# Group A attention: plain fp32 probabilities and values, weighed on two 64-column tiles of TensorE, without remainders

## The reference, cut to what matters

```
def _gqa_blocked(q, k, v):            # 8 query heads, 2 key/value heads, head size 64, blocks of 128 queries
    sc = jnp.einsum('bqkgd,bskd->bkgqs', qblk, k, preferred_element_type=jnp.float32) * scale
    p = jax.nn.softmax(sc, axis=-1).astype(v.dtype)
    return jnp.einsum('bkgqs,bskd->bqkgd', p, v)
```

## Time and profile before

| | before |
|---|---|
| median of 3 runs | 2302.78 us (2302.01 to 2313.93) |
| the profiled execution | 2301.58 us, its span 2299.8 us |
| mean granted PE clock | 0.982 of full speed |
| PE, DVE, ACT, POOL busy | 2200.8, 1622.3, 803.5, 291.9 us |
| group A, from the first exponential to that of group B's item 0 | 352.27 to 623.61 us |

### The profile page before, as it was taken

How to read it: one execution, slowest core, us unless ns; L and a number is a source line. 1 busy time by engine, 2 the same in 40 slices (tenths; PEclk the granted TensorE clock), 3 DMA queues, 4 the chain that set the end, 5 groups by cost and what they waited for, 6 DMA issues and landing times.

```text
span 2299.8 us, 30438 instructions
## 1 busy us (share of the span) xinstructions
PE 2200.8 (96%) x11036; PEld 1789.2 (78%) x11036; DVE 1622.3 (71%) x2168; ACT 803.5 (35%) x1298; POOL 291.9 (13%) x183
## 2 busy tenths in 40 slices
PE   7999999999998989999999999999999999987997
PEld 5777887777776778888888888888888888875885
DVE  6786527888877776568776777777777777766555
ACT  6222216777755562142212122222122212144223
POOL 6101001000000013410000000000000000014001
PEclk9999999999999989999999999999999999998998
DMA  5213356101255503101010100010110101010112
GB/s 171 106 73 133 118 165 151 28 15 26 50 110 116 112 2 146 36 28 37 28 36 27 36 30 34 30 33 27 36 36 27 36 27 36 28 55 19 37 37 110
DMA packets 51021, 137.48 MB, mean 60 GB/s; under 512 B 20240, under 2 KB 20752, under 8 KB 50960
## 3 DMA queue, kind: packets, MB, share of 16 engines
q1 hardware_dynamic: 50096, 135.55, 19.9%
q10 hardware_dynamic: 864, 1.13, 0.1%
HBM read 105.99 MB, written 30.67 MB: 59 GB/s over the span
## 4 chain that ended last, share of the span: by engine, by line
PE 83%; DVE 9%; ACT 2%; issue 2%; DMA 2%; POOL 1%; SPq 1%; DVEq 0%; ACTq 0%; POOLq 0%
PE ps L297 23%; PE ps L299 23%; PE ps L298 23%; PE ps L1008 3%; PE ps L984 3%; DVE nmax L1175 2%; PE ps L1022 2%; DMA TR<-in_rpb 2%; PE ps L973 2%; DVE PTL L1196 1%; PE ps L974 1%; DVE NL L1816 1%; PE ps L992 1%; POOL accx L459 1%; PE ps L495 1%
## 5 line engine op out<-in xcount | busy, mean ns | idle before, releaser
L297 PE MATMUL ps<-NH,WH 128*128 128x512 f32 x1896 | 756.1, 399 | 19.8 <-DVE WL L661 9.3
L298 PE MATMUL ps<-NL,WH 128*128 128x512 f32 x1896 | 742.2, 391 | 0.0
L299 PE MATMUL ps<-NH,WL 128*128 128x512 f32 x1896 | 742.2, 391 | 0.0
L297 PEld LDWEIGHTS ps<-NH,WH 128*128 128x128 f32 x1896 | 358.7, 189 | 106.9 <-DVE NL L655 16.0
L298 PEld LDWEIGHTS ps<-NL,WH 128*128 128x128 f32 x1896 | 358.7, 189 | 79.2 <-issue 6.0
L299 PEld LDWEIGHTS ps<-NH,WL 128*128 128x128 f32 x1896 | 358.1, 189 | 75.8
L1748 DVE TENSOR_TENSOR H<-H,ps 128x512 f32<-128x512 f32 x480 | 305.5, 683 | 101.0 <-PE ps L299 101.0
L274 POOL TENSOR_TENSOR raw<-raw,gains 128x1024 f32<-128x1024 f32 x76 | 152.2, 2008 | 1326.2 <-DMA raw<-in_w 1326.2
L289 ACT ACTIVATE WH<-raw 128x1024 fp32r<-128x1024 f32 x102 | 107.8, 1057 | 572.6 <-PE ps L299 543.2
L297 PE MATMUL ps<-MH,WH 128*128 128x512 f32 x504 | 197.9, 393 | 6.6 <-DVE H L1823 4.7
L984 PE MATMUL ps<-ident,PR 128*128 128x128 f32 (+1 forms) x1056 | 167.7, 286 | 32.5 <-DVE PF L1192 15.7
(11 more groups left out here) (174 smaller groups left out, 2715.3 us busy)
## 6 DMA issues: line engine op xcount, KB each, us to landing
raw<-in_w SPq DMA_DIRECT2D x102, 512.0 KB, 3.3
xst<-in_xT SPq DMA_DIRECT2D x24, 256.0 KB, 3.4
H<-in_xT SPq DMA_DIRECT2D x8, 768.0 KB, 8.8
out_yT<-H SPq DMA_DIRECT2D x24, 256.0 KB, 2.1
qkh<-oqh SPq DMA_DIRECT2D x5, 768.0 KB, 3.3
qkl<-oql SPq DMA_DIRECT2D x5, 768.0 KB, 4.9
qkh<-obh SPq DMA_DIRECT2D x5, 768.0 KB, 3.5
qkl<-obl SPq DMA_DIRECT2D x5, 768.0 KB, 5.9
```

The source lines that it names most:

```text
L297: nc.tensor.matmul(out, wh, xh, start=first, stop=False)
L298: nc.tensor.matmul(out, wh, xl, start=False, stop=False)
L299: return nc.tensor.matmul(out, wl, xh, start=False, stop=last)
```

## The change

Group A gets group B's way of storing: one array VA of values and one array PA of probabilities, both plain fp32, and no VT, PTH, PTL. ACT copies the first bank of turned probabilities, DVE the second, straight from PSUM, each once bank and engine are ready; the semaphores `t_hi` go. `weigh` runs one plain fp32 matmul for a key block, with 64 stationary columns and 256 streaming ones: even key blocks onto output partitions 0 to 63, odd ones onto 64 to 127. The read-out, which adds the two halves, stays. Group B's instructions stay as they are.

```
@@ weigh, PE
-                    for x in (PTH, PTL):
-                        mm = nc.tensor.matmul(ps[:, PVBANK, at:at + queries], VT[s][0:kn, k0 // P + kb, :],
-                                              x[0:kn, (m // 2) % 2, n, c0:c0 + queries],
-                                              start=(kb == 0 and x is PTH), stop=(kb == todo[-1][0] and x is PTL))
+                    mm = nc.tensor.matmul(ps[cols(kb % 2, DH), PVBANK, at:at + queries], VA[s][0:kn, k0 // P + kb, :],
+                                          PA[0:kn, (m // 2) % 2, n, c0:c0 + queries],
+                                          start=kb < 2, stop=kb >= todo[-1][0] - 1)
@@ values, ACT
-                for b in range(2):
-                    act.wait_ge(t_rdy[b], fills("A", p, ("V", s)))
-                    nc.scalar.activation(VT[s][:, 6 * b:6 * b + 6, 0:DH], value_src(b), ACT.Copy).then_inc(t_hi[b], 1)
+                act.wait_ge(t_rdy[0], fills(kind, p, ("V", s)))
+                nc.scalar.activation(VA[s][:, 0:6, :], value_src(0), ACT.Copy).then_inc(t_free[0], 1)
@@ step, ACT
-                if kind == "A":
-                    turned(kind, p, m, 1)
-                else:
-                    act.wait_ge(t_rdy[1], fills(kind, p, ("T", m)))
+                act.wait_ge(t_rdy[1], fills(kind, p, ("T", m)))
@@ turned (was turned_low), DVE
-                dve.wait_ge(t_hi[b], fills(kind, p, ("T", m)))
-                nc.vector.tensor_tensor(turned_dst(PTL, m, w, b), turned_src(b, len(split_blocks(w)[b])),
-                                        turned_dst(PTH, m, w, b).bitcast(F32), ALU.subtract).then_inc(t_free[b], 1)
+                dve.wait_ge(t_rdy[1], fills(kind, p, ("T", m)))
+                nc.vector.tensor_copy(turned_dst(PA, m, w, 1), turned_src(1, len(split_blocks(w)[1]))).then_inc(t_free[1], 1)
@@ values (was values_low), DVE
-                for b in range(2):
-                    dve.wait_ge(t_hi[b], fills("A", p, ("V", s)))
-                    nc.vector.tensor_tensor(VT[s][:, 6 * b:6 * b + 6, DH:P], value_src(b),
-                                            VT[s][:, 6 * b:6 * b + 6, 0:DH].bitcast(F32), ALU.subtract).then_inc(t_free[b], 1)
+                dve.wait_ge(t_rdy[1], fills(kind, p, ("V", s)))
+                nc.vector.tensor_copy(VA[s][:, 6:12, :], value_src(1)).then_inc(t_free[1], 1)
```

More of the change, by code:

```diff
@@ L190, in build @@
         value_home = c.at
-        VT = [c(f"VT{s}", [T // P, P], F32R) for s in range(2)]
+        VA = [nc.alloc_sbuf_tensor_at(f"VA{s}", [P, T // P, DH], F32, offset=value_home + 6 * KB * s) for s in range(2)]
+        c = Region(value_home + 12 * KB)
         probs_home = c.at
[L193 to L196, removed]
+        PA = c("PA", [2, TS // P, 2 * P])
         PR = c("PR", [2, TS])
@@ L774, in build @@
         s_rdy, m_done, e_done = sem("s_rdy"), sem("m_done"), sem("e_done")
-        t_rdy, t_hi, t_free = ([sem(f"{x}{b}") for b in range(2)] for x in ("t_rdy", "t_hi", "t_free"))
+        t_rdy, t_free = ([sem(f"{x}{b}") for b in range(2)] for x in ("t_rdy", "t_free"))
         ri_ok, r_rdy, pv_done, o_copy, o_sum, o_done, o_sq, o_acc = (
@@ L1022, in weigh_both @@
                         mm = nc.tensor.matmul(ps[cols(half, DH), PVBANK, cols((m // 2) % 2, P)],
-                                              VF[s][0:kn, windows[half][0] // P + kb, 0:DH],
-                                              PF[0:kn, (m // 2) % 2, n, cols(half, P)],
+                                              VA[s][0:kn, windows[half][0] // P + kb, 0:DH],
+                                              PA[0:kn, (m // 2) % 2, n, cols(half, P)],
                                               start=kb == 0, stop=kb == len(places(windows[half][1])) - 1)
@@ L1087, in turned @@
                 src = turned_src(b, len(split_blocks(w)[b]))
-                if kind == "B":
-                    nc.scalar.activation(turned_dst(PF, m, w, b), src, ACT.Copy).then_inc(t_free[b], 1)
-                else:
-                    nc.scalar.activation(turned_dst(PTH, m, w, b), src, ACT.Copy).then_inc(t_hi[b], 1)
+                nc.scalar.activation(turned_dst(PA, m, w, b), src, ACT.Copy).then_inc(t_free[b], 1)
             def out_copy(p, b):
@@ L1157, in table, with values @@
                     nc.vector.tensor_copy(TM[s][GRID:P, 1:NA_KH + 1, :], TE[s][GRID:P, 3:3 + NA_KH, :]).then_inc(tab[s], 1)
[L1159 to L1163, removed]
-                for b in range(2):
-                    dve.wait_ge(t_hi[b], fills("A", p, ("V", s)))
-                    nc.vector.tensor_tensor(VT[s][:, 6 * b:6 * b + 6, DH:P], value_src(b),
-                                            VT[s][:, 6 * b:6 * b + 6, 0:DH].bitcast(F32), ALU.subtract).then_inc(t_free[b], 1)
+            def values(kind, p, s):
+                dve.wait_ge(t_rdy[1], fills(kind, p, ("V", s)))
+                nc.vector.tensor_copy(VA[s][:, 6:12, :], value_src(1)).then_inc(t_free[1], 1)
             def row_max(kind, p, m):
@@ L1185, in row_max, with turned @@
                                                    accum_out=nmax[:, m:m + 1]).then_inc(m_done, 1)
-            def turned_low(kind, p, m, b):
+            def turned(kind, p, m):
                 _, w, _, _ = window(kind, m)
[L1190 to L1194, removed]
-                dve.wait_ge(t_hi[b], fills(kind, p, ("T", m)))
-                nc.vector.tensor_tensor(turned_dst(PTL, m, w, b), turned_src(b, len(split_blocks(w)[b])),
-                                        turned_dst(PTH, m, w, b).bitcast(F32), ALU.subtract).then_inc(t_free[b], 1)
+                dve.wait_ge(t_rdy[1], fills(kind, p, ("T", m)))
+                nc.vector.tensor_copy(turned_dst(PA, m, w, 1), turned_src(1, len(split_blocks(w)[1]))).then_inc(t_free[1], 1)
             def inverse(p, b):
@@ L1233, in step @@
                     if late:
-                        turned_low(kind, p, m, 1)
+                        turned(kind, p, m)
                     if after is None and m in (20, 21):
@@ L1241, in step @@
                     if not late:
-                        if kind == "A":
-                            turned_low(kind, p, m, 0)
-                        turned_low(kind, p, m, 1)
+                        turned(kind, p, m)
                     if m % 4 == 2:
@@ L1247, in step @@
                     if m == V1_AT and kind == "B":
-                        values_low("B", p, 1)
+                        values("B", p, 1)
                     if m == V0_AT and after == "B":
-                        values_low("B", p + 1, 0)
+                        values("B", p + 1, 0)
                     if m == 3 and before is None:
@@ L1262, in s2_vector @@
             row_max("A", 0, 0)
-            values_low("A", 0, 0)
+            values("A", 0, 0)
             row_max("A", 0, 1)
-            values_low("A", 0, 1)
+            values("A", 0, 1)
             every_pair(dve, step)
```

## The result

The changed kernel takes 2281.47 us (median of 7 runs, 2279.03 to 2292.16) against 2302.78 (7 runs, 2298.72 to 2313.93); the ratio is 0.9907, 95% interval 0.9884 to 0.9931. It is 0.9% faster, 21 us, where 26 were forecast.

The account below looks back on a forecast made before the run. DVE's remainders were taken to bound group A. PE's work of 59.3 plus 2.5 of waits gives 61.8 against 68.1 us a pair, 25 for four, and 1.5 at the attention's start: 2277 us, range 2265 to 2292.

Parts of the forecast that it names:

- PE's own work: PE's work without waits in a pair of group A: from 58.1 to 59.3 us, a weighing of eight blocks at 1.88.
- the exit: Cost in what follows a weighing on PE, when the tiles change back; the prediction's sum had no term for it.
- the waits: PE's waiting in a pair of group A, for osum and bank 5: from 10.0 to 2.5 us, bounds 0 and 6.
- the start: Start of the attention: one copy of the values each instead of DVE's remainders brings 1 to 3 us, taken as 1.5.
- the entry: Transposes ahead of each weighing take 0.17 us longer for the change of tiles, 8 us over 48 weighings.
- the turn to long items: Step where scores of long items begin: bank 5 is 0.25 us late, then weighing waits 0.45 for osum; 0.7 per half pair.
- The other blocks: Remaining weighings of a half pair in group A: osum some 0.1 us late at each of three.
- New waits in the place of the old: Rival, 13%: osum and bank 5 always behind the row maximum, PE at 64 to 66 us a pair, 2291 us.
- Tiles that do not overlap: Rival, 6%: group A's 256-column records stream one after the other, a weighing of eight blocks takes 3.7 us; 2338 us.
- A falling clock in group A: Rival, 7%: weighing on tiles brings group B's lower clock to group A, 3.4 us a pair; 2291 us.
- the full clock throughout: Group A before the change: PE was said to have the full clock in its pairs, 68.1 us each.
- The remainders bound group A: DVE's row maximum and two subtractions, 1.22 + 2 x 0.68 us in a long item, must end before both banks are free.

Follow-up runs that it names:

- a0_after_again: An execution of the same changed kernel in a later run; its first pair of group A takes 60.8 us at a granted clock of 0.94.
- The two halves run apart: Against the kernel before: old weighing with the new copies, 2276.25 us, ratio 0.9889; new weighing with the old copy-then-subtract of the banks, 2307.69 us, ratio 1.0033.

## Why the prediction was right, point by point

The time came out 21 us lower where 26 were forecast, within the range, and the mechanism held: the hand-over is the gain and PE's own work does not shrink. Three terms of the sum were off, the exit, the waits and the start.

*PE's own work: right in its parts, with one cost left out and one put at twice its size.* The weighing took 1.88 us as worked out from group B's row and the untiled fp32 row, the entry its 0.17. The two halves run apart give +1.0 us a pair for the weighing against +1.2 in the sum, but that the two are close is luck: the entry costs 1.0 and not 2.0, since in half the places PE waits for DVE anyway, and the exit costs 1.0 and not nothing. (The sum took scores at 1.00 and 0.56 also behind a weighing, where the kernel before needs 0.93 and 0.47; so against the sum's own 59.3 the exit adds only some 0.5.) The Trainium skill, page TensorEngine Tiling, section Key Properties, names a drain at a change of the tiling mode; the rows show a cost on the way out too, 0.06 us for reciprocals and 0.1 for scores.

*The waits: right in place and cause, too small in size.* The term was 2.5 us a pair; the trace has 3.2. The largest single one, at the turn to long items, came out at 0.8 and 0.7 against 0.7, and short items lost the 0.2 once in each half pair. The other blocks were put at 0.1 each: where the scores have already turned to short items, the weighing is due sooner and waits 0.5 (475.21 to 476.71 above, 1.50 instead of 0.96) and 0.3. The cause that was argued, osum and bank 5 both behind the row maximum, is what moving osum showed, from one wait to the other, and what handing the copy to ACT showed by shrinking both.

*The start: not confirmed.* The sum put 1.5 us on the start of the attention. The two profiled executions seem to grant it: the first pair with the start gave 7.3 us against 7.8. But 2.2 of the 7.3 are the clock's. With the clock at 0.95 and 0.94 the first pair gains 5.1, no more than the others. In the two halves run apart, both at that clock too, the weighing and the values' copies together cost the first pair 0.2 us where the other pairs lose 1.0, and the hand-over gives it 5.4 instead of 6.1: the shorter copies can be worth at most 0.8, and the rest of the pair takes it back. No run has them alone.

*The sum.* Four pairs of 6.3 us and 1.5 at the start make 26.5. The profiled executions differ by 21.7, since the first pair gained 2.2 by the clock and the start lay 1.1 later; with the execution of a0_after_again, whose first pair has the clock of the kernel before, it is 20.5. What is missing is the start's 1.5 and some 1.1 in each pair: 0.4 to 0.5 for the exit and 0.7 for the waits. (The last step of the sum, from 2275 to the median's 2277, adds 1.2 and comes to 2276.) DVE was put at 44 us a pair and stands at 45.8: two subtractions back to back take 1.28 us in the trace of the kernel before and not 2 x 0.68, so less was shed.

*The rivals.* New waits in the place of the old: 3.2 us of them a pair, against the 6 of that case. Tiles that do not overlap: not so, and the order of the matmuls decides less than the rival assumed. A falling clock in group A: the change did not bring it, but "the full clock throughout" was read from two pairs. The first pair has the lower level (1.2 GHz instead of 2.4) for some 7 us in the kernel before and in 9 of 13 executions of changed kernels, where the changed kernel has it in one of its three; all other pairs of group A are at 1.00 in each. In group B the clock differs from execution to execution at the same counts: the pair that took 53.4 us at 0.97 above takes 55.7 at 0.91 in a0_after_again. That is a part of what runs of one kernel differ by.

*The reading of the bound.* "The remainders bound group A" was right as a statement on the order of operations: take the remainders away, with the same weighing, and 6.1 us a pair are gone. DVE's sum of 57.8 of 68.1 us would not have shown it: a DVE of 56.0 in 63.2 costs PE next to nothing if the work stands in the right place. Which part of the old order held the banks, ACT's copy ahead of DVE's or the second operation on DVE, no run took apart.

## What to carry to other kernels

Giving each PSUM bank to one engine with one operation, instead of to two in turn (copy, then subtract), was worth 6 us of 68 here. The saving in matmuls was worth nothing: sixteen fp32r records of 256 columns start 0.12 us apart, and a plain fp32 matmul's two records 0.21 apart, which two tiles only bring back. Count what stands ahead of the operation that releases a bank, not the engine's busy share: 10 us more on DVE cost 0.3, and 4 us more in the six steps with a read-out cost 4. When a wait is removed by moving an operation forward, look at what it is moved past; moving work to the engine with room shrank both waits. A cost of PE's own that lies beside a wait is not seen until the wait goes. And before a pair is compared with a pair, compare their granted clocks: 2.2 us of the first pair's 7.3 were nothing else.

## What the runs showed of the hardware that was not expected

Matmuls on two column tiles of 64 need not alternate to overlap. In the order even, even, odd, odd a weighing of four key blocks takes 1.03 us, as in turn, and one of eight, in twos, 1.93 against 1.88; with four even ones ahead of four odd ones it takes 2.79, not the 3.6 of one after the other. This fits a matmul that may start two matmuls ahead of its turn on a free tile; more than two tiles were not tried.

The change of tiles costs at both ends, 0.17 us in the transposes ahead of a weighing and 0.06 to 0.1 in what follows it, and the first of these costs nothing where PE waits there anyway (1.50 us with it, 1.49 without).
